# A three-block transformer kernel: norm roots with tokens on partitions, rests one behind, and the sums in front of each norm by two sets of tokens

## The chip, the cores and the metric

The kernel runs on one core of a Trainium2 chip. The metric is the device time of one launch in microseconds (us); lower is better.

## The reference

There are 1024 tokens (`x`, batch 1) and 256 context tokens (`ctx`), with 1024 features each. A first block is followed by an even and an odd layer and a final norm. Cut to what matters here:

```
def rms_norm(x, g):
    return x * rsqrt(mean(x * x, -1) + 1e-6) * g
def modulate(x, cond, g, w, b):        # cond: c for the tokens, c_ctx for the context
    shift, scale, gate = split(silu(cond) @ w + b, 3)
    return rms_norm(x, g) * (1 + scale) + shift, gate

# first block
z = rms_norm(x, g_mix) @ w_in          # four branches are split off it
y_a = chunk_attention(rms_norm(aq), rms_norm(ak), av)           # 4 heads of 64
y_b = indexed_attention(rope(rms_norm(bq)), rope(rms_norm(bk)), bv, iq, rope(rms_norm(ik)), iw)
y_c = rglru(cx, cy)
x = x + (gates * (y_a, y_b, y_c) @ w_branch) @ w_out            # "wo"
gu = rms_norm(x, g_ffn) @ w_ffn_in
x = x + (silu(g) * u) @ w_ffn_out      # 2816 inner features: "fg", "fu", "fo"
# even layer
h, hc = modulate(x, c), modulate(ctx, c_ctx)                    # both give q, k, v and gates
y = (window_attention(8 heads), rms_norm(differential_attention(4 heads)) * 0.2) * silu(g)
x = x + gate * (y @ w_out);  ctx likewise                        # "eo"
# odd layer
h, hc = modulate(x, c), modulate(ctx, c_ctx)
y = (latent_attention(rms_norm(cq), rms_norm(ckv), kr), neighbourhood_attention(8 heads)) * silu(g)
x = x + gate * (y @ w_out)                                       # "oo"
return rms_norm(x, final_g)
```

## The kernel before

**Layout.** Activations lie with features on partitions: `X` is 8 tiles of 128 features by 1024 tokens, plus 256 of context. A projection of one output tile of 128 features takes its tokens in chunks, `CH1` (512, 512) or `CH2` (512, 512, 256), one PSUM bank each. Each product in fp32 is made of three passes (`matmul3`, L2137 to L2139), with the rounded part and the rest of weight and input: 24 matmuls for eight input tiles and 512 tokens. So every input needs its high part (ScalarE) and its rest (VectorE or GpSimd), and every weight tile of 128x1024 too: SP loads it into one of two raw tiles (L2910), ScalarE casts it (L2314), VectorE subtracts (L2481), into one of two slots. `w_get` brings the tile of the next use but one into the slots.

**Order.** `schedule` writes one list of steps in program order; each engine's program walks the whole list and does its part of every step, so an engine is in order throughout, and semaphores tie the engines. Banks 0 to 5 go round in turn (`take`); 6 and 7 are kept for the attentions. In the attentions, a Fill object draws steps of the next head's projections and norms (generators that yield after each piece) between scores and products.

**The norms.** Squares of X are made on ScalarE (L2322) as each output tile of the projection before is added to X (L2678, or L2680 with a gate), and summed over the tiles on VectorE (L2489): `Squares`. When the last tile is there, `norm_split` forms for every chunk a matmul of ones with the sum (L2170, fp32), which puts the mean into all 128 partitions, then a square root on ScalarE (L2325) and a reciprocal on VectorE (L2492), both 128 x 512:

```
p.add("mean", n=n, o=o, ones=ones, x=x, more=list(more), after=list(after), free=bank_free[b])
p.add("root", n=n, rs=rs, ps=ps, after=done, eps=epst[0:rs.shape[0], 0:1] if eps else None)
```

Then come the pieces, eight tiles for each chunk: scale on VectorE (L2501), high part on ScalarE (L2329 to L2335, with the shift where the norm is modulated), rest on VectorE (L2506, L2508) or GpSimd (L2878), by turns. The big norms of this kind are the first one, the feed-forward's (1272), the even layer's (2051) and the odd layer's (3200), all between one block of projections and the next. The context's squares for the even layer are taken behind the feed-forward norm (L2489, 128x256), its pieces with the even layer's norm.

`post` and `post_steps` do the per-head norms of 64 features for queries and keys in the same way (L2170, L2325, L2492, scale L2496), then the rotation (L2179) and the split. `finish_steps` does the norm of a differential head, 128 features by 1280 tokens, three chunks; there the sum has a second term, the squares of the softmax sums, which is added by ten 128x128 matmuls (L2172). The latent attention norms its query and key inputs with `norm_split`. The last norm is done after the last output tile (`final`, L2786 and L2901), with a store for each of 16 pieces.

**Feed-forward.** 22 inner tiles in groups, `FFN_GROUPS = [4, 4, 4, 4, 3, 3]`: for each inner tile the projections `fg` and `fu`, then for the group eight output tiles `fo`, added to X.

**Final projection.** `oo` takes eight input tiles; four of them (`early`) were split before, the other four are split just ahead of it from the last heads' results (`late`), and the projection waits for all.

## Time and profile before

| | |
|---|---|
| median of 3 runs | 4293.37 us (4292.48 to 4294.66) |
| profiled execution | 4297.19 us, span of the trace 4295.4 us |
| granted TensorE clock, mean | 0.923 of full speed |
| busy share | TensorE 83%, weight loads 68%, VectorE 54%, ScalarE 34%, GpSimd 7% |
| matmuls | 18492 |
| VectorE instructions | 3898 |

Times in the rows are microseconds from the span's start. PE is TensorE, PEld its weight load, DVE VectorE, ACT ScalarE, POOL GpSimd; L12 is line 12 of the kernel before; `m` stands for a tile in SBUF and `PS` for one in PSUM. A matmul in fp32 that is not one of `matmul3`'s has two records.

### The profile page before, as it was taken

The page shows a single profiled execution, that of the slowest core. Times are in us where ns is not written, and L with a number is a line of the kernel's source. Part 1 is how long each engine was busy: PE and PEld are TensorE (multiplying, and loading weights), DVE is VectorE, ACT ScalarE, POOL GpSimd, SP SyncE. Part 2 cuts the span into 40 slices and gives each one's busy share as a digit, 9 for nine tenths or more (in the row PEclk, how much of TensorE's full clock was granted, in tenths as well). Part 3 has the DMA queues.
Part 4 walks back from the last instruction along what each step waited for, and adds up shares of the span by engine and source line. Part 5 has one row for each costly group of instructions (what it writes and reads, how often), then busy time and mean ns, then how long its engine had stood idle before and what let it go on. Part 6 is the DMA issues. An engine that isn't in the chain of part 4 may idle for free. (4 is left out here: it accounts for less than half of the span.)

```text
span 4295.4 us, 44938 instructions
## 1 busy us (share of the span) xinstructions
PE 3577.7 (83%) x18492; PEld 2908.7 (68%) x18492; DVE 2309.3 (54%) x3898; ACT 1465.0 (34%) x2564; POOL 296.8 (7%) x379
## 2 busy tenths in 40 slices
PE   3799897786888999999698877877687888868877
PEld 2588775665676888888466665766575777756666
DVE  4899735655733222223565646666544556435654
ACT  3311344443222111112434534444323445324431
POOL 2111110000100000000100000000001000010000
PEclk9899999887998999999799989999798999988998
DMA  2034330001520111111201000000210100100111
GB/s 84 30 108 143 131 133 27 26 20 37 184 88 32 52 49 49 37 45 46 79 27 33 22 31 31 25 26 22 102 69 33 34 29 29 36 23 13 31 64 59
DMA packets 69292, 229.97 MB, mean 54 GB/s; under 512 B 8472, under 2 KB 12568, under 8 KB 69088
## 3 DMA queue, kind: packets, MB, share of 16 engines
q1 hardware_dynamic: 43056, 132.68, 9.3%
q0 software_dynamic: 22576, 81.85, 5.5%
q10 hardware_dynamic: 3456, 12.58, 0.7%
q8 instruction: 145, 2.38, 0.2%
q14 instruction: 59, 0.48, 0.0%
HBM read 180.42 MB, written 36.17 MB: 50 GB/s over the span
## 5 line engine op out<-in xcount | busy, mean ns | idle before, releaser
L2137 PE MATMUL PS<-m,m 128*128 128x512 f32 (+2 forms) x3560 | 1424.5, 401 | 280.4 <-DVE m L2481 55.3
L2138 PE MATMUL PS<-m,m 128*128 128x512 f32 (+2 forms) x3560 | 1379.8, 388 | 0.0
L2139 PE MATMUL PS<-m,m 128*128 128x512 f32 (+2 forms) x3560 | 1379.7, 388 | 0.0
L2137 PEld LDWEIGHTS PS<-m,m 128*128 128x128 f32 (+1 forms) x3560 | 688.6, 194 | 477.1 <-issue 99.9
L2139 PEld LDWEIGHTS PS<-m,m 128*128 128x128 f32 (+1 forms) x3560 | 688.1, 194 | 137.4
L2138 PEld LDWEIGHTS PS<-m,m 128*128 128x128 f32 (+1 forms) x3560 | 690.8, 194 | 120.2 <-issue 3.4
L2481 DVE TENSOR_TENSOR m<-m,m 128x1024 fp32r<-128x1024 f32 (+4 forms) x203 | 207.8, 1024 | 415.0 <-ACT m L2314 414.3
L2766 DVE TENSOR_TENSOR m<-PS,m 128x512 fp32r<-128x512 f32 x352 | 241.1, 689 | 289.3 <-ACT m L2408 288.8
L2408 ACT CAST m<-PS 128x512 fp32r<-128x512 f32 x352 | 205.8, 589 | 512.5 <-PE PS L2236 511.0
L2227 PE MATMUL PS<-m,m 64*128 64x256 f32 (+5 forms) x1968 | 255.6, 371 | 86.2 <-ACT m L2397 57.9
L2227 PEld LDWEIGHTS PS<-m,m 64*128 64x128 f32 (+1 forms) x1968 | 216.8, 200 | 131.1 <-ACT m L2397 73.4
L2314 ACT CAST m<-m 128x1024 fp32r<-128x1024 f32 (+4 forms) x235 | 213.1, 907 | 228.5 <-PE PS L2139 189.0
L2236 PE MATMUL PS<-m,m 128*128 128x128 f32 x1408 | 239.0, 297 | 57.6 <-DVE m L2757 16.0
L2244 PE MATMUL PS<-m,m 128*128 128x256 f32 x704 | 229.2, 345 | 30.7 <-ACT m L2408 15.3
L2236 PEld LDWEIGHTS PS<-m,m 128*128 128x128 f32 x1408 | 180.8, 152 | 103.2 <-DVE m L2766 19.1
L2340 ACT COPY m<-PS 128x512 f32<-128x512 f32 (+1 forms) x158 | 85.5, 543 | 368.8 <-PE PS L2139 368.6
L2397 ACT ACTIVATE m<-PS,m 128x256 f32<-128x256 f32 (+1 forms) x272 | 188.2, 702 | 28.9 <-DVE m L2698 28.9
L2245 PE MATMUL PS<-m,m 128*128 128x256 f32 x704 | 195.4, 297 | 0.0
L2244 PEld LDWEIGHTS PS<-m,m 128*128 128x128 f32 x704 | 145.8, 207 | 43.8 <-ACT m L2408 30.8
L2248 PE MATMUL PS<-m,m 128*128 128x256 f32 x704 | 155.5, 304 | 23.5 <-DVE m L2766 23.1
L2678 DVE TENSOR_TENSOR m<-m,PS 128x512 f32<-128x512 f32 x112 | 76.8, 687 | 180.5 <-PE PS L2139 163.1
L2322 ACT ACTIVATE m<-m 128x512 f32<-128x512 f32 (+1 forms) x133 | 77.5, 594 | 280.1 <-DVE m L2680 169.7
(202 smaller groups left out, 3968.3 us busy)
## 6 DMA issues: line engine op xcount, KB each, us to landing
m<-in_w SPq DMA_DIRECT2D x220, 512.0 KB, 3.3
g_scratch<-m ACTq DMA_DIRECT2D x24, 512.0 KB, 2.6
m<-g_scratch POOLq DMA_DIRECT2D x24, 512.0 KB, 4.7
m<-in_w SPq DMA_DIRECT2D x32, 256.0 KB, 2.6
x_scratch<-m POOLq DMA_DIRECT2D x2, 4096.0 KB, 12.3
m<-m POOLq DMA_DIRECT2D x60, 128.0 KB, 2.7
y_scratch<-m POOLq DMA_DIRECT2D x12, 512.0 KB, 3.0
m<-y_scratch POOLq DMA_DIRECT2D x12, 512.0 KB, 5.4
```

The lines of the kernel that those rows point to most:

```text
L2137: pe.e.engine.matmul(o, L[0], X[0], start=start, stop=False)
L2138: pe.e.engine.matmul(o, L[0], X[1], start=False, stop=False)
L2139: return pe.e.engine.matmul(o, L[1], X[0], start=False, stop=stop)
L2227: m = e.matmul(o, L, X, start=first, stop=last)
L2236: m = e.transpose(PS[:, s["out"] + 128 * i:s["out"] + 128 * i + 128], x, ident)
L2244: e.matmul(O, vh, h, start=g == 0 and i == 0, stop=False)
L2245: e.matmul(O, vl, h, start=False, stop=False)
L2314: e.copy(s["hi"], s["src"]).then_inc(*act.says(S.hi, ("w", s["i"])))
L2397: m = e.activation(d, src if bias is None else d, ACT.Exp, bias=sums[:, 0:1], scale=scale, accum_out=sums[:, 3 + a:4 + a])
L2408: e.copy(s["h"], s["src"]).then_inc(*act.says(S.hi, ("pt", s["u"], s["g"])))
L2481: e.tensor_tensor(s["lo"], s["src"], s["hi"].bitcast(F), ALU.subtract).then_inc(*dve.says(S.lo, ("w", s["i"])))
L2766: e.tensor_tensor(s["l"], s["src"], s["h"].bitcast(F), ALU.subtract).then_inc(*dve.says(S.lo, ("pt", s["u"], s["g"])))
```

## The change

- **Roots with tokens on partitions.** A step "cols" takes 128 tokens of the summed squares as weights and one moving column of constants, so that 128 means land on 128 partitions in one column; root and reciprocal then work on 128 x 4 (or 8, or 10) columns. A step "rows" spreads them again: the column, repeated over 128 columns, is the weight, and the identity moves, which gives a 128x128 block with the roots in every partition. Scale instructions read it from PSUM (banks 6 and 7 for the big norms). All norms are done so, the last and the differential heads' too (there with both terms in the column).
- **Pieces on VectorE and ScalarE.** No rest is left on GpSimd; the shift always goes with the cast; the rest of a piece is issued behind the scale of the next one ("normlo"). The sum of squares is likewise one behind ("sumsq"). The last norm is all on VectorE.
- **Two sets of tokens.** `two_passes` runs the eight output tiles in front of a norm (`wo`, the last `fo` group, `eo`, `oo`) first for tokens 0 to 511 (for `eo` with the context), then again for 512 to 1023, so these weight tiles are loaded and split twice (`weight_order`, 32 more); between the tiles of the second pass the pieces of the first set are issued, two for a tile (three for `eo`). `split_pair` starts the two projections behind the norm on the finished set, issues the second set's columns and pieces at given marks, then finishes both.
- The context's squares and norm for the even layer move between the feed-forward's projections; the groups become [3, 3, 4, 4, 4, 4]; X is loaded in ten parts in place of two (nine in place of eight for `oo`); `oo` takes its early inputs first and waits for each late one alone; the differential heads' fill has one step more.

Cut to its core:

```diff
-FFN_GROUPS = [4, 4, 4, 4, 3, 3]
+FFN_GROUPS = [3, 3, 4, 4, 4, 4]
...
+TWICE = ["wo7", f"fo{len(FFN_GROUPS) - 1}_7", "eo7", "oo7"]
+def weight_order():
+    order = []
+    for tile in weight_tiles():
+        if tile[0][:2] not in ("ea", "oa"):
+            order.append(tile)
+        if tile[0] in TWICE:
+            order += order[-8:]
+    return order
...
-    def linear_steps(name, rhs, chunks, evac, rows=P, banks=None):
-        get, kt, release, split_w = w_get(name)
+    def linear_steps(name, rhs, chunks, evac, rows=P, banks=None, ahead=2, ks=None):
+        get, kt, release, split_w = w_get(name, ahead)
         for n, (t0, tn) in enumerate(chunks):
             b = take(banks)
             o = bank(b)[0:rows, 0:tn]
-            for k in range(kt):
+            for i, k in enumerate(ks or range(kt)):
...
+    def two_passes(jobs, first, then, side, each, **kw):
+        for name, rhs, evac in jobs:
+            linear(name, rhs, first, evac, **kw)
+        for n, (name, rhs, evac) in enumerate(jobs):
+            linear(name, rhs, then, evac, **kw)
+            for _ in range(each if n else 1):
+                next(side, None)
+        finish(side)
...
+    def load_x(X, src, context):
+        t = {(k, 0): move(X[:, k, 0:512], src[k][:, 0:512]) for k in range(8)}
+        c = move(X[:, :, T:TC], ctxT.rearrange("k p t -> p k t")) if context else None
+        e = move(X[:, :, 512:T], src.rearrange("k p t -> p k t")[:, :, 512:T])
+        for k in range(8):
+            t[k, 512], t[k, T] = e, c
+        return t
+    def split_pair(jobs, first, side, marks):
+        done = 0
+        gens = [linear_steps(name, h_rhs, chunks, evac, ahead=2 - n) for n, (name, chunks, evac) in enumerate(jobs)]
+        for n, g in enumerate(gens):
+            for i in range(8 * first[n]):
+                if done == marks[0]:
+                    next(side)
+                if done == marks[1]:
+                    finish(side)
+                done += 1
+                next(g)
+        for n, g in enumerate(gens):
+            for _ in g:
+                pass
+            if n == 0:
+                w_prep(st["use"] + 1)
...
             self.n += 1
-            p.add("square", n=n, x=x, q=self.sq[i][:, 0:tn], r=r, after=list(after) + self.free[i], before=self.t[c])
-            self.t[c] = self.free[i] = [(S.sumsq, n)]
+            p.add("square", n=n, x=x, q=self.sq[i][:, 0:tn], r=None, after=list(after) + self.free[i])
+            self.behind = n, c, i, r, self.sq[i][:, 0:tn]
+        def flush(self):
+            if self.behind:
+                n, c, i, r, q = self.behind
+                self.behind = None
+                p.add("sumsq", n=n, q=q, r=r, before=self.t[c])
+                self.t[c] = self.free[i] = [(S.sumsq, n)]
...
+    def roots(b, tiles, after, width=1, eps=True, at_=None):
+        s = rc_n[0] % 4
+        rc_n[0] += at_ is None
+        d = rc[:, 8 * s:8 * s + width * len(tiles)] if at_ is None else at_[:, 0:width * len(tiles)]
         n = p.id()
-        p.add("mean", n=n, o=o, ones=ones, x=x, more=list(more), after=list(after), free=bank_free[b])
-        return (S.mean, n)
-    def root(rs, ps, b, done, eps=True):
-        n = p.id()
-        p.add("root", n=n, rs=rs, ps=ps, after=done, eps=epst[0:rs.shape[0], 0:1] if eps else None)
+        o = bank(b)[:, 0:width * len(tiles)]
+        p.add("cols", n=n, parts=[(o[:, width * y:width * y + width], terms) for y, terms in enumerate(tiles)],
+              after=list(after), free=bank_free[b])
+        p.add("root", n=n, rs=d, ps=o, eps=epst[:, 0:1] if eps else None, free=rc_free[s] if at_ is None else [])
         bank_free[b] = [(S.root, n)]
-        return (S.recip, n)
-    def norm_split(src, kt, ones, chunks, g, shift, ready, hi, lo, bufs, sums=None):
-        sq, rs, tmp = bufs
+        return n, d, s, width, at_ is None
+    def spread(b, of, y0, tn, m=P):
+        n, d, s, width, shared = of
+        parts = []
+        for y in range(tn // 128):
+            for x in range(width):
+                i, w_ = width * (y0 + y) + x, m // width
+                parts.append((bank(b)[w_ * x:w_ * x + w_, 128 * y:128 * y + 128], d[:, i:i + 1].to_broadcast([P, w_])))
+        x = p.id()
+        p.add("rows", n=x, parts=parts, after=(S.recip, n), free=bank_free[b])
+        if shared:
+            rc_free[s] = [(S.rows, x)]
+        return bank(b)[0:m, 0:tn], (S.rows, x)
...
-        means = []
-        for c, (t0, tn) in enumerate(chunks):
-            b = take()
-            o = bank(b)[:, 0:tn]
-            means.append((b, o, mean(o, ones, rs[c][:, 0:tn], sums.t[c], b)))
-        root_t = [root(rs[c][:, 0:tn], means[c][1], means[c][0], means[c][2]) for c, (t0, tn) in enumerate(chunks)]
-        n, out_events, tmp_free = 0, {}, [[] for _ in tmp]
+        sums.flush()
+        root_of, n = {}, 0
+        chunks = [(c, t0, tn) for c, (t0, tn) in enumerate(chunks) if only is None or c in only]
+        for c, t0, tn in chunks:
+            root_of[c] = roots(take(), by_tiles(rs[c], tn, ones[:, 0:1]), sums.t[c])
+        yield
+        low = []
+        def rest_of():
+            m, key, how = low.pop(0)
+            p.add("normlo", n=m, **how)
+            tmp_free[how["i"]] = out_events[key] = [(S.lo, m)]
+        for c, t0, tn in chunks:
+            b = 6 + norm_n[0] % 2
+            norm_n[0] += 1
+            r, root_t = spread(b, root_of[c], 0, tn)
             for k in range(kt):
                 i = n % len(tmp)
                 sh = shift(k, c) if shift else None
                 m = p.id()
-                p.add("normed", n=m, q=tmp[i][:, 0:tn], x=src(k, t0, tn), g=g(k, c), r=r, sh=sh, how=how, on=on,
-                      hi=hi(k, t0, tn), lo=lo(k, t0, tn), after=[root_t[c]] + tmp_free[i] + ready(k))
-                tmp_free[i] = out_events[k, t0] = [(S.lo if on == "dve" else S.lo_g, m)]
+                q, h = tmp[i][:, 0:tn], hi(k, t0, tn)
+                p.add("normed", n=m, q=q, x=src(k, t0, tn), g=g(k, c), r=r, sh=sh, hi=h,
+                      after=[root_t] + tmp_free[i] + ready(k))
+                low.append((m, (k, t0), {"q": q, "hi": h, "lo": lo(k, t0, tn), "sh": sh, "i": i}))
                 n += 1
-        return out_events
+                if len(low) > 1:
+                    rest_of()
+                if k == kt - 1:
+                    rest_of()
+                yield
+            bank_free[b] = [(S.scale, m)]
...
-                c["m"] = mean(c["o"], cc("o64", c["rows"], c["rows"]), c["x"], [(S.square, n)], c["b"])
+                c["of"] = roots(take(), by_tiles(c["x"], c["tn"], heads(c["rows"])), [(S.square, n)], c["rows"] // 64)
...
-                t = root(c["x"], c["o"], c["b"], c["m"])
+                b = take()
+                r, t = spread(b, c["of"], 0, c["tn"], c["rows"])
                 n = p.id()
-                p.add("scale", n=n, z=c["z"], g=c["gain"][0:c["rows"], :], r=c["x"], after=[t] + c["t"])
-                c["t"] = [(S.scale, n)]
+                p.add("scale", n=n, z=c["z"], g=c["gain"][0:c["rows"], :], r=r, after=[t] + c["t"])
+                bank_free[b] = c["t"] = [(S.scale, n)]
...
+        two_passes([(f"wo{d}", h_rhs, add_to(d, sums)) for d in range(8)], CH1[0:1], CH1[1:2], ffn_norm(0), 2)
...
+                if f0 + f == 0:
+                    split_pair([("fg0", CH1, ev_g), ("fu0", CH1, ev_u)], (1, 1), late_norm(), (3, 7))
+                else:
+                    linear(f"fg{f0 + f}", h_rhs, CH1, ev_g)
+                    linear(f"fu{f0 + f}", h_rhs, CH1, ev_u)
+                if context:
+                    next(context, None)
...
+                two_passes([(f"fo{n}_{d}", u_rhs, add_to(d, sums)) for d in range(8)], CH1[0:1], CH1[1:2],
+                           modulated("ev", bufs, sums, [0]), 2)
...
+        split_pair([("ek", k_first, ek), ("eq0", k_first, eq)], (2, 2), rest, (8, 12))
...
+                of = roots(take(banks), [[(zq[:, 128 * y:128 * y + 128], cc("o128")[:, 0:1]), (ident, squares[h % 2][:, y:y + 1])]
...
+        two_passes([(f"eo{d}", h_rhs, add_gated(d, sums)) for d in range(8)], CH2[0:1] + CH2[2:3], CH2[1:2],
+                   modulated("od", bufs, sums, [0, 2]), 3)
...
+        split_pair([("dq0", CH1, dq), ("dk0", k_first, dk)], (1, 2), rest, (4, 8))
...
+        def final_steps(c):
+            t0, tn = CH1[c]
+            sums.flush()
+            of = roots(take(), by_tiles(rs[c], tn, cc("o1024")[:, 0:1]), sums.t[c])
+            yield
+            r, t = spread(6 + c, of, 0, tn)
             for k in range(8):
+                p.add("final", n=(k, c), x=X[:, k, t0:t0 + tn], r=r, g=vc("fin_g", k), after=t,
                       out=out[k][:, t0:t0 + tn])
+                yield
+        two_passes([(f"oo{d}", y_rhs, add_gated(d, sums)) for d in range(8)], CH1[0:1], CH1[1:2], final_steps(0), 2,
+                   ks=early + [0, 1, 2, 3])
+        finish(final_steps(1))
...
-        elif s.kind == "mean":
+        elif s.kind == "cols":
...
-            m = e.matmul(s["o"], s["ones"], s["x"], start=True, stop=not s["more"])
-            for i, (o, L) in enumerate(s["more"]):
-                m = e.matmul(o, L, ident, start=False, stop=i == len(s["more"]) - 1)
+            for o, terms in s["parts"]:
+                for i, (L, X) in enumerate(terms):
+                    m = e.matmul(o, L, X, start=i == 0, stop=i == len(terms) - 1)
+        elif s.kind == "rows":
+            pe.wait_ge(*s["after"])
+            for ev in s["free"]:
+                pe.wait_ge(*ev)
+            for o, L in s["parts"]:
+                m = e.matmul(o, L, ident, start=True, stop=True)
+            m.then_inc(*pe.says(S.rows, s["n"]))
...
+        elif s.kind == "normlo":
+            dve.wait_ge(S.hi, n)
+            if s["sh"] is None:
+                e.tensor_tensor(s["lo"], s["q"], s["hi"].bitcast(F), ALU.subtract).then_inc(*dve.says(S.lo, n))
+            else:
+                e.scalar_tensor_tensor(out=s["lo"], in0=s["q"], scalar=s["sh"], in1=s["hi"].bitcast(F), op0=ALU.add,
+                                       op1=ALU.subtract).then_inc(*dve.says(S.lo, n))
...
-        elif s.kind == "normed" and s["on"] == "pool":
-            pool.wait_ge(S.hi, n)
-            e.tensor_tensor(s["lo"], s["q"], s["hi"].bitcast(F), ALU.subtract).then_inc(*pool.says(S.lo_g, n))
```

## Rows read from the trace of the kernel before

**Rows 1.** The page, part 1: busy us, share of the span, instructions.

```profile
PE 3577.7 (83%) x18492; PEld 2908.7 (68%) x18492; DVE 2309.3 (54%) x3898; ACT 1465.0 (34%) x2564; POOL 296.8 (7%) x379
```

**Rows 2.** Stretches: length, busy us and records of PE, PEld, DVE, ACT, POOL; clock; DMA, GB/s.

```profile
698.00:1060.00 362.00, 288.12 (x1532) 225.39 (x1531) 221.97 (x460) 170.82 (x316) 19.32 (x50) 0.87 0.06 20
1060.00:1190.00 130.00, 99.71 (x422) 81.65 (x421) 86.01 (x115) 27.82 (x35) 20.02 (x36) 0.87 0.53 189
1190.00:1272.00 82.00, 82.00 (x363) 67.90 (x362) 27.64 (x35) 16.04 (x22) 0.00 (x0) 1.00 0.26 93
1272.00:1322.00 50.00, 25.75 (x54) 13.52 (x53) 32.23 (x34) 18.93 (x31) 12.49 (x10) 0.61 0.00 0
1322.00:2051.00 729.00, 715.14 (x3120) 588.83 (x3119) 214.15 (x285) 129.82 (x193) 0.00 (x0) 0.99 0.15 47
2051.00:2110.00 59.00, 30.50 (x79) 18.94 (x80) 38.86 (x45) 28.05 (x47) 13.97 (x13) 0.65 0.21 80
2520.00:3063.00 543.00, 415.78 (x2496) 345.21 (x2496) 342.09 (x585) 242.89 (x501) 17.07 (x34) 0.92 0.10 31
3200.00:3254.00 54.00, 20.04 (x54) 11.59 (x53) 36.06 (x42) 25.57 (x44) 14.50 (x14) 0.70 0.19 78
```

**Rows 3.** Timeline of VectorE at the end: start, us, instruction, [idle before].

```profile
4263.65 0.75 DVE L2680 SCALAR_TENSOR_TENSOR m<-PS,m,m 128x512 f32<-128x512 f32 x1 [3.30 <-PE PS L2139]
...
4269.09 0.75 DVE L2680 SCALAR_TENSOR_TENSOR m<-PS,m,m 128x512 f32<-128x512 f32 x1 [3.30 <-PE PS L2139]
...
4285.30 6.17 DVE L2786 SCALAR_TENSOR_TENSOR m<-m,m,m 128x512 f32<-128x512 f32 x6
```

**Rows 4.** Timeline of VectorE behind the first block's output projection.

```profile
1275.59 6.56 DVE L2492 RECIPROCAL m<-m 128x512 f32<-128x512 f32 x2 [1.31 <-ACT m L2325]
...
1312.48 0.69 DVE L2506 TENSOR_TENSOR m<-m,m 128x512 fp32r<-128x512 f32 x1 [0.69 <-ACT m L2329]
...
1320.34 1.23 DVE L2481 TENSOR_TENSOR m<-m,m 128x1024 fp32r<-128x1024 f32 x1 [0.51 <-ACT m L2314]
```

**Rows 5.** Groups by form: instruction xcount | busy us, mean ns | idle before.

```profile
L2314 ACT CAST m<-m 128x1024 fp32r<-128x1024 f32 x172 | 179.6, 1045 | 82.3 <-PE PS L2139 43.7 <-DMA m<-in_w 19.7 <-issue 11.6
L2481 DVE TENSOR_TENSOR m<-m,m 128x1024 fp32r<-128x1024 f32 x140 | 171.3, 1224 | 328.9 <-ACT m L2314 328.7
...
L2492 DVE RECIPROCAL m<-m 128x512 f32<-128x512 f32 x38 | 126.6, 3344 | 49.1 <-ACT m L2325 49.0
...
L2759 DVE RECIPROCAL m<-m 128x1 f32<-128x1 f32 x160 | 25.9, 162 | 10.9 <-ACT m L2397 6.8
...
L2680 DVE SCALAR_TENSOR_TENSOR m<-PS,m,m 128x512 f32<-128x512 f32 x32 | 23.9, 751 | 101.8 <-PE PS L2139 75.3 <-DMA m<-in_ctxT 17.7 <-DMA m<-x_scratch 8.8
...
L2492 DVE RECIPROCAL m<-m 128x256 f32<-128x256 f32 x7 | 12.1, 1724 | 0.1
L2496 DVE SCALAR_TENSOR_TENSOR m<-m,m,m 128x512 f32<-128x512 f32 x16 | 12.0, 752 | 0.6
```

**Rows 6.** Timeline of TensorE, narrow matmuls in fp32 at three places.

```profile
522.17 1.84 PE L2206 MATMUL PS<-m,m 128*128 128x2 f32 x16
...
2798.37 1.12 PE L2170 MATMUL PS<-m,m 128*128 128x512 f32 x2 [1.62 <-ACT m L2322]
2799.33 1.05 PE L2172 MATMUL PS<-m,m 128*128 128x128 f32 x8
...
3068.27 1.91 PE L2172 MATMUL PS<-m,m 128*128 128x128 f32 x8
```

**Rows 7.** Timeline of TensorE in the first attention.

```profile
967.99 1.12 PE L2179 MATMUL PS<-m,m 128*128 128x512 f32 x2 [4.09 <-DVE m L2496]
```

**Rows 8.** Timeline of VectorE in the last feed-forward group.

```profile
2041.25 0.55 DVE L2481 TENSOR_TENSOR m<-m,m 128x384 fp32r<-128x384 f32 x1
...
2045.70 0.55 DVE L2481 TENSOR_TENSOR m<-m,m 128x384 fp32r<-128x384 f32 x1
```

**Rows 9.** The page, part 6: count, KB each, median us from issue to landing.

```profile
m<-in_w SPq DMA_DIRECT2D x220, 512.0 KB, 3.3
```

More of the change, by code:

```diff
@@ L857, in w_get @@
         w_load(i + NRAW)
-        w_prep(i + 2)
+        w_prep(i + ahead)
         if i not in parts:
@@ L935, in norm_split, with by_tiles, norm_steps @@
+    def by_tiles(x, tn, X):
+        return [[(x[:, 128 * y:128 * y + 128], X)] for y in range(tn // 128)]
+    norm_n = [0]
+    def norm_split(*args, **kw):
+        out_events = {}
+        for _ in norm_steps(out_events, *args, **kw):
+            pass
+        return out_events
+    def norm_steps(out_events, src, kt, ones, chunks, g, shift, ready, hi, lo, bufs, sums=None, only=None):
+        sq, rs, tmp, tmp_free = bufs
         if sums is None:
@@ L1411, in evac @@
                 x = X[:, d, t0:t0 + tn]
-                p.add("addx", n=n, x=x, o=o, gate=None, after=[done] + t_x)
+                p.add("addx", n=n, x=x, o=o, gate=None, after=[done, t_x[d, t0]])
                 if sums:
```

222 lines of the change are left out of this document (102 added, 120 removed).

## The prediction

> **What bounds the kernel now.** I read the page's first part, then a table of stages, then the timelines of the stages in which TensorE stands still. TensorE is busy for 3577.7 us of 4295.4 [rows 1], so an edit pays only where it closes one of its gaps. The stage table [rows 2] shows where they are. The largest are three boundaries between a block of projections and the next one, at 1272, 2051 and 3200 us: in 50, 59 and 54 us TensorE has 54, 79 and 54 records, of which 48, 72 and 48 are projection work (4, 6 and 6 are the sums' matmuls; the odd ones are neighbours). A projection of 512 tokens by 1024 inputs is 24 matmuls and takes 5.44 us (the distance of two adds that each wait for one, [rows 3]), so the work done in those stretches is 10.9, 13.6 and 10.9 us, and 39, 45 and 43 us are lost. The granted clock there is 0.61 to 0.70, that is, part of the work runs at 1.2 GHz; I put that at 2.6 us for each restart (an estimate: half of 5.3 us in which the restarted projection runs at half pace).
>
> What fills the gaps is VectorE. At 1275.59 two reciprocals of 128x512 take 6.56 us, then come sixteen pieces until 1312.48, then the context's squares, and only at 1320.34 the rest of the next weight, behind which the second projection stands [rows 4]. The reciprocal costs 3344 ns for 512 columns and 1724 for 256, against 0.69 to 0.75 us for every other pass over 512 columns; 47 of them are 145 us of VectorE [rows 5].
>
> **The sums of a norm.** Before, ones(128x128) times the squares gives a full 128x512 sum, rooted (0.69 us) and inverted (3.35). Now four matmuls with one moving column put tokens on partitions, root and reciprocal work on 4 to 10 columns, and four 128x128 matmuls with a constant row spread them. The nearest rows: a pair of records for a matmul with two columns is 2 x 0.115 = 0.23 us (sixteen records in 1.84), a 128x128 matmul in the same number format is 0.26 us at full clock and 0.48 at half [rows 6]. So four columns are 0.9 to 1.0 us, four rows 1.05 to 1.9. Root and reciprocal on a few columns: the reciprocal of one column is 162 ns [rows 5]; I take 0.2 each; bounds 0.15 and 0.7. The chain is thus 2.5 to 3.4 us in place of 2.0 (old matmul, cold) + 0.7 + 3.35, and VectorE gets back 3.2 per chunk.
>
> Where this lies open on the path:
> - Start: two chunks, one behind the other, VectorE setting the pace: 2.2 each, 4. The rests that GpSimd did go to VectorE, which no longer stalls behind it: even.
> - The indexer's key norm: two reciprocals in a row, 5.
> - The first attention's queries and keys (670 to 698): four in a row, 13.4 us (4 x 3.34), and the scores wait for the splits queued behind them. What replaces them ends with the value projection on TensorE (rows 4.3 us longer there): 8.
> - The latent norms (3770 to 3822): five reciprocals (14.8 us), less two spreads at half clock: 10.
> Together 27.
>
> In the attentions twelve chunks are normed between the scores (698 to 1060). VectorE works in order, so each reciprocal holds softmax work: TensorE waited 4.09 us behind the scale that follows one [rows 7], and 2 to 4 behind others. Against it: TensorE now waits itself at the spread until root and reciprocal are through, and does 1.1 us more per chunk. Net 1.7 of 3.35, for twelve 20; bounds 0 and 35. In the differential heads (2520 to 3063) each norm has 8.4 us of reciprocals. Against them stand 20 column matmuls (4.7) and ten rows (2.6) in place of two and a half wide matmuls at 0.96 and ten narrow ones, 5.0 together: 2.3 more, which leaves 6.1. The heads' stream is in places TensorE's own already, so I take a little over half: 3.5 for each of three heads, 3 for the last. Together 34; bounds 5 and 55.
>
> Removed from GpSimd: all rests and the final norm's share; its queue is left with moves. One load of X becomes ten. Nobody waits for them: six banks hold 32 us of projections, and the adds' wait of 17.7 us for the context's load [rows 5] fell between 1190 and 1272, where TensorE was busy for 82 us of 82 [rows 2].
>
> **Two passes at the boundaries.** `two_passes` does all eight output tiles for the first 512 tokens, then all again for the second, with the first half's norm pieces behind the tiles of the second pass. `split_pair` then starts the next two projections on the finished half, while the second half is normed.
> The second half: from the last projection, add 0.75, the sum one behind 0.7, square 0.63, the next weight's two parts in the same queues (1.04 and 1.23, [rows 5]), last sum 0.69: 5 us to the columns, 0.4 to the reciprocal, rows behind the fourth to seventh step, then eight pieces at 1.45 to 1.5 us (scale 0.75, rest 0.7 to 0.75, the cast between them covered because the rest is one behind): done at 21 to 22 us. TensorE has 16.3 us of ready work (19.0 with context) plus 2 of sums, and the last projection can only follow its last piece by 0.7. It loses 6.5, 4 and 4 us.
> The second pass: a tile has one chunk, so 5.44 us of matmuls for a weight of 1.04 + 1.23. VectorE per tile: weight 1.23, add and sum 1.44, two pieces 2.9: 5.6 us, on the edge. Behind a finished tile stand add, sum, pieces, cast, rest until the tile after next may start, 6.6 us: (6.6 + 5.44) / 2 = 6.0 a tile, for four tiles 2.4 us. After the differential layer three pieces go behind a tile: 7.2 a tile, falling to 5.9 with the context's short ones: 6. In the feed-forward's last group (four inputs blocks now, was three) a tile is only 2.72 us and VectorE has 5.1: 9.5 for four tiles, plus 1 of small gaps; before, that group also went at VectorE's pace (4.45 us from one weight rest to the next, [rows 8], against 18 matmuls or 4.08), 3 us.
> Boundaries: 41.6 - 6.5 - 2.4 = 32; 48 + 3 - 4 - 10.5 = 36; 46.3 - 4 - 6 = 36. The columns and rows of the first halves and of the context stand in TensorE's stream, five times 2: -8 (part is hidden where VectorE leads). The context's norm itself moves beside the feed-forward's projections, where VectorE is busy for 214 us of 729 [rows 2]; its two table changes fall on ScalarE's idle time. Without that cover it would be 12.
> 32 more weight tiles on SP's queue: a load lands in 3.3 us [rows 9], and the stage from 1060 moved 189 GB/s [rows 2]; 512 KB in 5.44 us are 96. Nothing, as long as a tile's load, cast and rest stay under 8.6 us (below).
>
> **The last norm.** The final projection starts with the four inputs that are split already and takes the others as they come: 5. After the last add at 4269.09 now follow square, sum, columns, root, rows (4.7 us) and eight scales at 0.7; from the last scale to the end I keep the 3.9 us of before (4291.5 to 4295.4, [rows 3]): the end at 4283.5 for 4295.4, 12.
>
> **Sum.** 27 + 34 + 32 + 36 + 36 - 8 + 5 + 12 = 174 us. The profiled execution took 4297.2 us (1.8 around its span): 4123. The median is 3.8 lower: **4119**.
>
> One price is disputed. The pieces now read the roots from PSUM. The rows with one operand in PSUM and with none are 751 and 752 ns for the same instruction [rows 5], so I charge nothing. The Trainium skill (VectorE: DVE Perf Modes, "The TRN2 errata") gives VectorE 62 cycles more for a PSUM source than for an SBUF one, 65 ns; by an estimate from that page some 130 instructions would lose 8 us, and the time would be 4127 at most. The trace disagrees, and it decides.
>
> **Rivals.**
> A. The attentions keep their waits: TensorE stands at each spread as long as it stood behind the reciprocals. For it: it is in order, and root and reciprocal queue behind exponentials and table loads. Against: 3.35 us of VectorE are gone in any case. 4119 + 34 = 4153. 0.15.
> B. The passes starve. All first-half pieces lie open, because the next weight's rest stands behind them: 24 x 1.45 + 8 x 0.95 = 42 us against the 18 charged: 4143. The stage rows speak for it only in the short last group. 0.10.
> C. More than summed: the attentions give 55, and the restarts at half clock vanish with every short gap: 4090. 0.09.
> D. Slower. Weights come too late for tiles of one chunk. There are 56 such tiles; 174 / 56 = 3.1 us more for each would eat everything, that is 8.6 us per weight, 61 GB/s. The loads' 3.3 us and 189 GB/s speak against. At 10 us a tile the time would be 4370. 0.02.
> E. The halves depend on each other by some wait that I overlooked, so that pieces start after the second pass, and the longer stream of TensorE takes the rest: about 4290. 0.02.
>
> **How the numbers follow.** The forecast has 0.62, its own range 4100 to 4140 (bounds of the attention term and of the pass terms). To leave out no more than 2 in 10 the range takes in most of A, B and C: 4085 to 4162. What this measurement can tell from no change is about 0.2%, 9 us. Faster: forecast, A, B, C, 0.96; same 0.02 (E); slower 0.02 (D).
>
> **What would show it.** No reciprocal over 10 columns under the norms' line; VectorE's busy time down by some 80 us (145 less, rests from GpSimd and weights added); 32 more weight loads of 512 or 256 KB; TensorE's gap at each boundary under 8 us; in the feed-forward's second pass VectorE over 90% for four tiles; after the last projection's end 14 us. Wrong if TensorE waits for a weight's rest in the second passes for more than 20 us in all, or if the spreads in the attentions show waits of 3 us each.

## The result, and the profile after

The changed kernel takes **4178.57 us** (median of 4 runs, 4178.2 to 4181.32) against 4293.48 us; the ratio is 0.9734, 95% interval 0.9717 to 0.9751. That is 115 us less, where 174 were forecast: the right sign, and 4178.6 lies 17 us above the upper end of the range, 4162. The profiled execution has a span of 4176.9 us and took 4178.5.

The page's first part after the change answers to [rows 1]:

```profile
PE 3620.3 (87%) x19222; PEld 2990.5 (72%) x19222; DVE 2210.9 (53%) x3974; ACT 1449.1 (35%) x2556; POOL 242.2 (6%) x344
```

TensorE has 730 records and 42.6 us more than before, and 161 us less of gaps. VectorE fell by 98 us (80 were forecast), in spite of the weights' and pieces' rests it took over.

Stretches after the change (columns as in [rows 2]): the first boundary, the second pass of the last feed-forward group, the second boundary, the differential heads, the final projection's second pass, and the end.

```profile
1248.00:1262.00 14.00, 11.14 (x44) 9.07 (x43) 4.38 (x8) 2.76 (x5) 0.00 (x0) 0.76 0.18 64
1980.00:2012.00 32.00, 24.70 (x107) 18.53 (x108) 23.97 (x37) 14.80 (x23) 0.04 (x1) 0.95 0.22 71
2012.00:2023.00 11.00, 9.41 (x52) 8.10 (x52) 3.01 (x6) 2.21 (x4) 0.84 (x1) 0.84 0.98 357
2443.00:2986.00 543.00, 437.73 (x2601) 370.25 (x2599) 318.47 (x579) 236.20 (x493) 16.98 (x34) 0.88 0.10 31
4104.00:4162.00 58.00, 47.02 (x176) 36.58 (x174) 19.89 (x26) 9.56 (x12) 0.00 (x0) 0.87 0.25 82
4162.00:4177.00 15.00, 3.94 (x16) 3.56 (x16) 7.54 (x12) 0.89 (x2) 0.00 (x0) 0.56 0.37 140
```

The boundaries are closed: 14 and 11 us with 11.1 and 9.4 of TensorE busy, where before 50 and 59 us held 25.8 and 30.5. The end is 15 us. But the last projection's second pass takes 58 us for eight tiles that need 43.5, and the heads' clock is 0.88 where the stage of [rows 2] had 0.92.

To see where the forecast went, one goes through both traces by marks that both have (the last add in front of a norm, the first score of an attention), and takes the lead of the new kernel at each mark.

| up to | before | after | gained in stage | forecast |
|---|---|---|---|---|
| first projection | 65.8 | 55.7 | 10.0 | 4 |
| first top-k step | 171.9 | 160.3 | 1.6 | 5 |
| first attention, first score | 697.6 | 683.5 | 2.5 | 8 |
| its last score | 1042.3 | 1013.5 | 14.7 | 20 |
| last add of `wo` | 1272.2 | 1247.4 | -4.0 | -2.4 |
| last add of the feed-forward | 2053.6 | 2011.0 | 17.8 | 27.6 |
| window attention, first score | 2149.2 | 2068.7 | 37.9 | 44 |
| differential heads, first score | 2515.3 | 2438.8 | -4.0 | 0 |
| their last score | 3049.7 | 2972.8 | 0.4 | 10.5 |
| last add of `eo` | 3199.6 | 3131.0 | -8.3 | -3 |
| neighbourhood attention, first score | 3288.7 | 3179.8 | 40.3 | 42.3 |
| latent attention, first score | 3872.2 | 3753.0 | 10.3 | 10 |
| last add of `oo` | 4269.1 | 4162.0 | -12.1 | 5 |
| end of the span | 4295.4 | 4176.9 | 11.4 | 12 |

(The 8 us for columns and rows stand apart in the forecast.) Three stages make most of the difference: `oo`, 17; the feed-forward with its last group, 10; the heads, 10.

**The final projection.** SP's queue in its second pass, start, us of issue and instruction; and ScalarE's timeline there:

```profile
4113.54 1.00 SPq L3053 DMA_DIRECT2D out<-m  x2
4114.59 0.47 SPq L3046 DMA_DIRECT2D m<-in_w  x1
4122.73 0.99 SPq L3053 DMA_DIRECT2D out<-m  x2
4123.77 0.46 SPq L3046 DMA_DIRECT2D m<-in_w  x1
```

```profile
4118.49 1.04 ACT L2461 CAST m<-m 128x1024 fp32r<-128x1024 f32 x1 [5.20 <-DMA m<-in_w]
...
4127.48 1.04 ACT L2461 CAST m<-m 128x1024 fp32r<-128x1024 f32 x1 [5.36 <-DMA m<-in_w]
```

L3053 are the stores of the last norm's pieces for tokens 0 to 511, L3046 a weight load. Each load is issued only behind two stores, and these wait for scales that come behind the tile's add. The load goes out at 4114.59 and ScalarE waits for it 5.20 us until 4118.49; the tile behind it starts late, and so do its scales and the next load. Four tiles go at 9.0 us.

**The heads.** TensorE's timeline at the column step of the first and of the last head:

```profile
2577.90 6.66 PE L2312 MATMUL PS<-m,m 128*128 128x1 f32 x40 [2.45 <-ACT m L2469]
...
2990.33 8.69 PE L2312 MATMUL PS<-m,m 128*128 128x1 f32 x40 [4.40 <-ACT m L2469]
```

And the granted clock from there on (stretch, length, busy us and records, clock, DMA):

```profile
2578.00:2580.00 2.00, 2.00 (x19) 1.00 0.04 8
2580.00:2582.00 2.00, 2.00 (x12) 0.54 0.00 0
2582.00:2584.00 2.00, 2.00 (x12) 0.50 0.00 0
2600.00:2602.00 2.00, 0.97 (x4) 0.84 0.00 0
2602.00:2604.00 2.00, 2.00 (x11) 1.00 0.00 0
```

20 matmuls with one column (40 records) take 6.66 to 8.69 us, where I had 4.7. At the first head the clock falls to 1.2 GHz at 2580, 2 us into this step, with TensorE busy for 2.00 of 2 us on both sides of the fall (it had waited 2.45 us ahead of the step), and comes back at 2600. At the last head it is at half already ahead of the step (0.52 from 2979 to 2990).

**The last feed-forward group.** VectorE and ScalarE in its first pass:

```profile
1961.90 0.69 DVE L2623 TENSOR_TENSOR m<-m,m 128x512 fp32r<-128x512 f32 x1 [1.27 <-ACT m L2461]
1962.51 0.68 DVE L2820 TENSOR_TENSOR m<-m,PS 128x512 f32<-128x512 f32 x1
1963.11 0.69 DVE L2631 TENSOR_TENSOR m<-m,m 128x512 f32<-128x512 f32 x1
1965.06 0.69 DVE L2623 TENSOR_TENSOR m<-m,m 128x512 fp32r<-128x512 f32 x1 [1.27 <-ACT m L2461]
```

```profile
1963.88 0.63 ACT L2469 ACTIVATE m<-m 128x512 f32<-128x512 f32 x1 [2.02 <-DVE m L2631]
1964.42 0.60 ACT L2461 CAST m<-m 128x512 fp32r<-128x512 f32 x1
```

A tile is 2.72 us of matmuls and goes at 3.16 to 3.22. The square (L2469) waits 2.02 us for the sum of the tile before (L2631), since there is one buffer for squares and the sum now comes one add later; the next weight's cast (L2461) stands behind it, and that weight's rest (L2623) waits 1.27 us for the cast.

### The profile page after: what moved, and what is told of

Read it like the earlier page. It is cut to its first block and busy times, and to the rows that moved or that the text cites. A ratio compares the mean times of both kernels' runs of the same rounds, so it can differ in the third digit from the quotient of the medians.

```text
span 4176.9 us, 46529 instructions
## 1 busy us (share of the span) xinstructions
PE 3620.3 (87%) x19222; PEld 2990.5 (72%) x19222; DVE 2210.9 (53%) x3974; ACT 1449.1 (35%) x2556; POOL 242.2 (6%) x344
## 3 DMA queue, kind: packets, MB, share of 16 engines
q1 hardware_dynamic: 47664, 147.36, 10.8%
## 5 line engine op out<-in xcount | busy, mean ns | idle before, releaser
L2278 PEld LDWEIGHTS PS<-m,m 128*128 128x128 f32 (+1 forms) x3560 | 688.4, 194 | 118.5 <-issue 1.7
L2623 DVE TENSOR_TENSOR m<-m,m 128x1024 fp32r<-128x1024 f32 (+4 forms) x235 | 244.7, 1042 | 474.9 <-ACT m L2461 474.3
L2461 ACT CAST m<-m 128x1024 fp32r<-128x1024 f32 (+3 forms) x267 | 242.5, 908 | 197.8 <-PE PS L2279 132.3
L2391 PE MATMUL PS<-m,m 128*128 128x256 f32 x704 | 223.5, 338 | 34.3 <-ACT m L2553 15.8
L2383 PEld LDWEIGHTS PS<-m,m 128*128 128x128 f32 x1408 | 175.5, 148 | 90.2 <-DVE m L2908 19.3
L2542 ACT ACTIVATE m<-PS,m 128x256 f32<-128x256 f32 (+1 forms) x272 | 188.0, 702 | 19.4 <-DVE m L2840 19.3
L2392 PE MATMUL PS<-m,m 128*128 128x256 f32 x704 | 191.2, 292 | 0.0
L2391 PEld LDWEIGHTS PS<-m,m 128*128 128x128 f32 x704 | 141.8, 201 | 46.6 <-ACT m L2553 34.1
L2469 ACT ACTIVATE m<-m 128x512 f32<-128x512 f32 (+1 forms) x133 | 77.3, 594 | 269.5 <-DVE m L2631 147.6
L2835 DVE TENSOR_REDUCE m<-PS 128x1 f32<-128x1024 f32 x96 | 116.6, 1219 | 101.9 <-PE PS L2374 101.9
L2395 PE MATMUL PS<-m,m 128*128 128x256 f32 x704 | 153.8, 302 | 15.9 <-DVE m L2908 15.8
```

Source lines behind the costliest of these rows:

```text
L2278: pe.e.engine.matmul(o, L[0], X[1], start=False, stop=False)
L2383: m = e.transpose(PS[:, s["out"] + 128 * i:s["out"] + 128 * i + 128], x, ident)
L2391: e.matmul(O, vh, h, start=g == 0 and i == 0, stop=False)
L2392: e.matmul(O, vl, h, start=False, stop=False)
L2461: e.copy(s["hi"], s["src"]).then_inc(*act.says(S.hi, ("w", s["i"])))
L2542: m = e.activation(d, src if bias is None else d, ACT.Exp, bias=sums[:, 0:1], scale=scale, accum_out=sums[:, 3 + a:4 + a])
```

## The experiments

Each starts from the changed kernel (4178.6 us). The runs of one kernel lie 3 to 16 us apart, and stages that an edit doesn't touch differ by 4 to 5 us too (the window attention's took 366 to 371 us in all of them), so I read stages beside medians.

**e1: the stores elsewhere.**

```diff
-        elif s.kind == "final":            # SP
+        elif s.kind == "final" and s["n"][1] == 1:
...
+        elif s.kind == "final" and s["n"][1] == 0:      # GpSimd
+            pool.wait_ge(S.outd, s["n"])
+            e.dma_start(s["out"], s["x"]).then_inc(*pool.says(S.out_g, "stored"))
```

> Edit: the changed kernel, but the last norm's eight stores for tokens 0 to 511 are issued by GpSimd and not by SP. Theory: in the final projection's second pass SP issues each weight load only behind two of these stores (loads at 4114.59, 4123.77, 4132.76 and 4141.79, each 1.05 us behind the first store), so that four tiles take 9.0 us where a tile without stores takes 5.5. Freed of them the four should take 5.5 to 6: 12 to 14 us less, 4165 to 4167 us, and no wait of ScalarE for the weight's load there. Rival: VectorE's and ScalarE's order between scale, add and weight sets the pace, the late load is only where it shows: 4176 to 4180 us.

Measured: 4165.7 us, ratio 0.9702 (0.9688 to 0.9716). From the first to the last add of `oo` it takes 87.6 us for 106.8, 19 less, while the spans of the two profiled executions differ by 16 and the medians by 13. Of the 19, 3 lie in the tile with the columns, ahead of the first of these stores: it takes 8.2 us for 11.3, at a granted clock of 1.00 for 0.70. ScalarE in the same place:

```profile
4113.63 0.63 ACT L2469 ACTIVATE m<-m 128x512 f32<-128x512 f32 x1 [4.99 <-DVE m L2822]
4114.17 1.04 ACT L2461 CAST m<-m 128x1024 fp32r<-128x1024 f32 x1
4120.06 0.63 ACT L2469 ACTIVATE m<-m 128x512 f32<-128x512 f32 x1 [4.85 <-DVE m L2822]
4120.60 1.04 ACT L2461 CAST m<-m 128x1024 fp32r<-128x1024 f32 x1
```

The casts no longer wait. The cause is shown.

**e2: one matmul for the heads' second term.**

```diff
-  of = roots(take(banks), [[(zq[:, 128 * y:128 * y + 128], cc("o128")[:, 0:1]), (ident, squares[h % 2][:, y:y + 1])]
-                           for y in range(10)], [(S.square, n), squares_done[h]], eps=False, at_=inverse)
+  of = roots(take(banks), [[(zq[:, 128 * y:128 * y + 128], cc("o128")[:, 0:1])] for y in range(10)],
+             [(S.square, n), squares_done[h]], eps=False, at_=inverse, wide=(ident, squares[h % 2][:, 0:10]))
...
+  m = e.matmul(*s["wide"], start=True, stop=False)
```

> Edit: the changed kernel, but in the differential heads the second term of the sums (the squares of the softmax sums) is added by one matmul with ten moving columns, and not by ten with one: 11 matmuls in place of 20 in each head's column step. Theory: a column matmul costs 0.33 us here (40 records in 6.66 us), and the granted clock falls to half inside this step (at 2580, TensorE being busy), so each of four heads gives back 3 us and some of the stretch at half clock: 12 to 18 us less, 4161 to 4167 us. Rival: the columns lie beside other waits of the head (the mean of the heads' gaps hides them): 4175 to 4180 us.

Measured: 4163.2 us, 0.9691 (0.9675 to 0.9708), 15 us less. TensorE at the first head's column step:

```profile
2581.98 0.39 PE L2311 MATMUL PS<-m,m 128*128 128x10 f32 x2 [2.45 <-ACT m L2472]
2582.22 2.61 PE L2315 MATMUL PS<-m,m 128*128 128x1 f32 x20
```

The step takes 2.85 us for 6.7 there, and 4.9 in the other heads, where it runs at half clock. From the heads' first score to the last add of `eo` it is 680.2 us for 693.0.

**e3: the heads' norm as before the change.**

```diff
-  r, t = spread(b, of, t0 // 128, tn)
+  p.add("mean", n=m, o=bank(b)[:, 0:tn], ones=cc("o128"), x=r, after=[(S.square, n), squares_done[h]],
+        free=bank_free[b], more=[(bank(b)[:, 128 * y - t0:128 * y - t0 + 128],
+                                  squares[h % 2][:, y:y + 1].to_broadcast([P, P])) for y in tiles])
+  p.add("root", n=m, rs=r, ps=bank(b)[:, 0:tn], eps=None, free=[])
```

> Edit: the changed kernel with the differential heads' norm made as before (a 128x512 mean by a ones matmul and ten narrow ones, root and reciprocal over the full width). Theory: the heads gained nothing by the change (the stage from the first to the last of their scores took 534.4 us before and 534.0 after), so this should be within 4 us of the changed kernel: 4174 to 4183 us. Rival, the predicted price: the columns are worth 13.5 us there, so 4190 to 4194 us.

Measured: 4181.1 us, 0.9737 (0.9723 to 0.9752), the same as the changed kernel; the stage is 691.7 us for 693.0. So at 20 matmuls a head the columns bring nothing, and at 11 (e2) some 12 us (680.2 against 691.7). The mean clock from the heads to `eo` is 0.91 here, 0.86 in the changed kernel and 0.87 in e2, with TensorE busy for 432, 463 and 450 us.

**e4: one pass in front of every norm.**

```diff
-TWICE = ["wo7", f"fo{len(FFN_GROUPS) - 1}_7", "eo7", "oo7"]
+TWICE = []
...
+        if jobs[-1][0] not in TWICE:
+            for name, rhs, evac in jobs:
+                linear(name, rhs, first + then, evac, **kw)
+            finish(side)
+            return
```

> Edit: the changed kernel, but the projections in front of the four norms run in one pass for all tokens, as before; the norm's pieces for the first tokens come behind the last tile, and the pair of projections behind it is still started on them. Theory: the passes cost about what they save. With one pass the boundaries lose 16, 18 and 23 us (6.5 us to the roots, then 16, 16 and 24 pieces at 1.26 to 1.41 us, less the projections they run beside) and the last norm 5, 62 in all; with two passes they lose 12, 20, 15 and 18, 65 in all. So 4165 to 4190 us. Rival, the predicted prices: the passes save what they were charged with, 41 us lost against 62 and more: 4200 us or more.

Measured: 4164.0 us, 0.9698 (0.9683 to 0.9712): **faster than with two passes**, by 15 us, and the intervals don't meet. It is 1 us below the range that I had expected. `split_pair` is still there: the first two projections still start on the first tokens while the others are normed. By stages, in us:

| stage | two passes | one pass | e1 |
|---|---|---|---|
| `wo`, first to last add | 87.9 | 82.3 | 87.9 |
| from there to the first `fo` add | 78.3 | 84.7 | 78.4 |
| `fo`, first to the last group's last add | 685.4 | 670.5 | 688.8 |
| from there to the window attention | 57.0 | 67.9 | 57.1 |
| `eo`, first to last add | 115.0 | 105.6 | 118.5 |
| from there to the neighbourhood attention | 48.0 | 63.7 | 46.4 |
| `oo`, first to last add | 106.8 | 83.8 | 87.6 |
| from there to the end | 14.2 | 19.3 | 13.1 |

The passes save 6.4, 10.9, 15.7 and 5.1 behind the four norms, 38 in all, and cost 5.6, 14.9, 9.4 and 23.0 in front of them, 53. Only `eo` gains, by 6; `wo` is even, the feed-forward's group loses 4, and `oo`, once its stores are out of the way (e1), is 2 us better with two.

**e5: the first attention's norms as before the change.**

```diff
-  r, t = spread(b, c["of"], 0, c["tn"])
+  p.add("mean", n=m, o=o, ones=cc("o64"), x=c["x"], after=[c["sq"]], free=bank_free[b], more=[])
+  p.add("root", n=m, rs=c["x"], ps=o, eps=epst[:, 0:1], free=[])
...
-  p.add("scale", n=n, z=c["z"], g=c["gain"], r=r, after=[t] + c["t"])
+  p.add("scale", n=n, z=c["z"], g=c["gain"], r=c["x"], after=[(S.recip, m)] + c["t"])
```

> Edit: the changed kernel, but the twelve chunks of queries and keys that are normed between the first attention's scores are done as before (full-width mean, root and reciprocal, scale from SBUF). Theory: the columns there are worth what the two traces show between the first and the last of that attention's scores, 14.7 us: 4191 to 4195 us. Rival (TensorE stands at the spreads as long as it stood behind the reciprocals, and the stage gained for other reasons): 4178 to 4183 us.

Measured: 4189.3 us, 0.976 (0.9746 to 0.9775): 11 more, 2 below the range expected. The interval touches that of the changed kernel, so the stage has to decide. From this attention's first score to `wo`'s first add it is 490.6 us for 476.7, 13.9 us, near the 14.7 of the theory; the rest lies in stages that the edit doesn't touch.

**e6: each rest at once.**

```diff
-                if len(low) > 1:
-                    rest_of()
-                if k == kt - 1:
-                    rest_of()
+                rest_of()
```

> Edit: the changed kernel, but the rest of each piece of the big norms is issued right behind its own scale, and not behind the next one's. Theory: VectorE then stands for each cast (0.7 us of wait in each piece, as between the pieces before the change), so the eight open pieces behind each of three boundaries take 2.0 to 2.1 us in place of 1.26 to 1.41, 17 us together, and the second passes, where VectorE is at its edge, lose 5 to 15 more: 4200 to 4212 us. Rival: TensorE has enough ready work to cover it: 4179 to 4188 us.

Measured: 4219.7 us, 0.9828 (0.9813 to 0.9842): 41 more, above my theory's 21 to 33. VectorE behind the first boundary, and the same place in the changed kernel:

```profile
1272.46 0.69 DVE L2645 TENSOR_TENSOR m<-m,m 128x512 fp32r<-128x512 f32 x1 [0.69 <-ACT m L2475]
1273.07 0.74 DVE L2640 SCALAR_TENSOR_TENSOR m<-m,m,PS 128x512 f32<-128x512 f32 x1
1274.50 0.69 DVE L2645 TENSOR_TENSOR m<-m,m 128x512 fp32r<-128x512 f32 x1 [0.69 <-ACT m L2475]
1275.11 0.74 DVE L2640 SCALAR_TENSOR_TENSOR m<-m,m,PS 128x512 f32<-128x512 f32 x1
```

```profile
1251.49 0.68 DVE L2631 TENSOR_TENSOR m<-m,m 128x512 f32<-128x512 f32 x1
1254.31 0.18 DVE L2634 RECIPROCAL m<-m 128x4 f32<-128x4 f32 x1 [2.14 <-ACT m L2474]
1260.25 1.41 DVE L2643 SCALAR_TENSOR_TENSOR m<-m,m,PS 128x512 f32<-128x512 f32 x2 [5.76 <-PE PS L2319]
1261.68 0.69 DVE L2648 TENSOR_TENSOR m<-m,m 128x512 fp32r<-128x512 f32 x1
1262.29 0.74 DVE L2643 SCALAR_TENSOR_TENSOR m<-m,m,PS 128x512 f32<-128x512 f32 x1
1262.95 0.68 DVE L2648 TENSOR_TENSOR m<-m,m 128x512 fp32r<-128x512 f32 x1
```

A piece takes 2.04 us for 1.26. I had left out the start: the first projection begins at 67.4 and not at 55.7, 11.7 us. From the last add of `wo` to the last of the feed-forward it is 14.4 us more, in `eo` 11.8, behind it 7.0.

**e7 and e8: put together.** Both have the edits of e1 and e2. e7 takes the last feed-forward group out of the two passes:

```diff
-TWICE = ["wo7", f"fo{len(FFN_GROUPS) - 1}_7", "eo7", "oo7"]
+TWICE = ["wo7", "eo7", "oo7"]
```

> Edit: the stores on GpSimd, the single matmul for the heads' second term, and the last feed-forward group in one pass. Theory: the first two add up (13 and 15.4 us), and one pass there gives 4 more (14.9 less in the group, 10.9 more behind it, by the trace of the kernel with one pass everywhere): 4143 to 4149 us. Rival: the gains overlap: 4153 us or more.

Measured: **4134.6 us**, 0.9637 (0.9622 to 0.9651), 44 less than the changed kernel, and 8 below the lower end of what I expected. By stages against the changed kernel: the heads with `eo` 13 less, `oo` 19, the feed-forward 16 less and the boundary behind it 10 more. The 6 us that are left are stages that it shares with the others (2 ahead of `wo`, 4 in the window attention).

e8 leaves the two passes there, and gives the squares a second buffer:

```diff
+  bufs = bufs[0], bufs[1], bufs[2][0:3], bufs[3][0:2] + [list(sg_free[0])]
+  sums.sq, sums.free = [bufs[0][0], sg[1]], [sums.free[0], list(sg_free[1])]
```

> Edit: the stores on GpSimd, the single matmul for the heads' second term, and the last feed-forward group in two passes, but with a second buffer for the squares (and three for the pieces in place of four). Theory: with one buffer a square waits for the sum of the one before (2.02 us of wait at each square there), the next weight's cast waits behind it, and the weight's rest behind that, which makes 3.17 us of a tile of 2.72 in the first pass and 5.17 in the second. With two the first pass falls to 2.75 and the second by 0.5 to 1 a tile: 6 to 8 us less than without, 4142 to 4145 us. Rival: another link of the loop holds it, 4148 to 4152 us.

Measured: 4138.1 us, 0.964 (0.9624 to 0.9656), 4 below the range expected, which rested on the same estimate as e7's. VectorE in the group's first pass, for the rows at 1961.90 above:

```profile
1961.41 0.69 DVE L2627 TENSOR_TENSOR m<-m,m 128x512 fp32r<-128x512 f32 x1 [0.61 <-ACT m L2465]
1962.28 0.69 DVE L2824 TENSOR_TENSOR m<-m,PS 128x512 f32<-128x512 f32 x1 [0.18 <-PE PS L2280]
1962.89 0.69 DVE L2635 TENSOR_TENSOR m<-m,m 128x512 f32<-128x512 f32 x1
1964.17 0.69 DVE L2627 TENSOR_TENSOR m<-m,m 128x512 fp32r<-128x512 f32 x1 [0.60 <-ACT m L2465]
```

The tile goes at 2.76 to 2.95, mean 2.86, and the square no longer waits for the sum: that link is shown. The second pass stays at 5.17 with its two pieces, where VectorE has seven instructions and one wait for a cast, so the group gained 2.6 us and not 6 to 8. As a total it can't be told from e7.

**e9: one pass and each rest at once** (the edits of e4 and e6).

> Edit: one pass in front of all four norms, and the rest of each piece right behind its own scale. What of the change is left is the narrow roots, and that VectorE does all rests. Theory: the order of the rests is worth as much with one pass as with two (41 us there): 12 at the start, 0.7 for each of 16, 16 and 24 open pieces, 39, so 4164 + 51 = 4215 us, 4208 to 4222, and again no more than with two passes (4219.7). Rival: slow pieces are where the two passes pay, because more of them lie open in one pass: 4232 us or more.

Measured: 4211.1 us, 0.9801 (0.9787 to 0.9816). So the order of the rests is worth 47 us with one pass and 41 with two, and even with slow pieces the passes don't pay (4211 against 4220). The expectation says that only the narrow roots and the rests on VectorE are left of the change; that is too little. Also left are `split_pair`, the sum of squares one behind, the loads of X in ten parts, the feed-forward's groups and `oo`'s early inputs.

**e10: e7 with `wo` in one pass too.**

```diff
-TWICE = ["wo7", "eo7", "oo7"]
+TWICE = ["eo7", "oo7"]
```

> Edit: as the best so far (stores on GpSimd, single matmul, last feed-forward group in one pass), and the first block's output projection in one pass too. Theory: in the trace with one pass everywhere this projection took 5.6 us less and the stage behind it 6.4 more, so nothing changes: 4132 to 4138 us. Rival: with VectorE freed in front, one pass is better there as well: 4128 us or less.

Measured: 4140.4 us, 0.9634 (0.9618 to 0.965): 2 us above the range, and by its ratio the same as e7. By stages `wo` takes 82.9 us for 87.9 in e7, and from there to the first `fo` add it is 83.7 for 78.2. Even, as e4's stages said.

## Why the prediction was wrong

Taken apart by e9, e4 and the changed kernel, the change is: all that e9 leaves of it (narrow roots, rests on VectorE, `split_pair` and the small parts), 82 us (4293.5 to 4211.1); rests one behind, 47 (to 4164.0); two passes, **minus 15** (to 4178.6). The 82 are not taken apart further: e5 shows 14 of them as narrow roots in the first attention, e3 none in the heads, and no run is without `split_pair`. The forecast of the boundaries themselves came near (37.9 for 44 and 40.3 for 42.3); what stands in front of them was priced far too low, and what closes them was not told apart.

**The step that failed: the price and the worth of the passes.** The sum charged the second passes 2.4, 10.5, 6 and nothing, 19 us. Against one pass they cost 5.6, 14.9, 9.4 and 23.0, 53 us (e4): 34 of the 60 us that the forecast missed. The heads are 10 more. The prediction's own sign came, more than 20 us of TensorE waiting for a weight's rest in the second passes: 1.2, 6.0, 4.6 and 10.9, 22.7 in all. What the passes save, 38, does not pay for it. I had set 39, 45 and 43 us of loss before against what two passes would leave, and never priced the same boundary with one pass and the new pieces. (Of the terms, the third boundary's 46.3 should be 45.7 by the prediction's own numbers; the 36 stands.) I had the numbers: a piece at 1.45 us where before three took 5.8 (one piece in three held by GpSimd's rest). With the 1.26 us measured (e6's rows), sixteen pieces are 20 us, and 11 of these run beside the first two projections, which `split_pair` starts early. Most of what I credited to the passes, the pieces and `split_pair` give without them.

**The final projection, forecast 5, measured -12.** I charged its second pass nothing, neither the 2.4 and 6 us that I charged the others, nor its queue. I counted the loads of a second pass and found them harmless by their rate (96 of 189 GB/s); but the rate was not the limit. SP is in order, the pieces' stores are SP's too, and a load behind a store waits for a scale: 16 us in the tiles behind, 13 in the whole (e1). Rival D had weights that come too late, and had it for all 56 tiles by bandwidth; it happened in four, by order.

**The differential heads, forecast 10.5, measured 0.4.** The reciprocals went, 8.4 us a head. The term that was mis-sized is the columns: 0.23 us each from a row at full clock [rows 6], 0.33 measured and up to 0.43, because the clock is at half for 4.4 of the 6.66 us at the first head, and for all of the 8.69 at the last. I had looked at both clocks for the rows and at one for the columns. With nine matmuls fewer (e2) the stage takes 525.7 us, 9.1 less than before, near the forecast.

The columns are not needed to bring the clock down. At the first head of e2 it falls 2 us behind the start of the step, as in the changed kernel, but at the third it falls inside the wait, which ends at 2864.48 with the step's first matmul. TensorE in e2 there, and in e3, where the same norm has waits of 1.63, 1.21 and 0.99 us between wide matmuls until 2591:

```profile
2862.00:2864.00 2.00, 0.03 (x2) 1.00 0.00 0
2864.00:2864.40 0.40, 0.00 (x0) 0.61 0.00 0
```

```profile
2583.00:2592.00 9.00, 5.56 (x30) 1.00 0.01 2
```

So a wait of 2.45 us was enough without a column, and with the shorter waits the clock stayed up through the sums. Whether the columns add to it is open.

**The last feed-forward group, forecast -7.5, measured -13.9.** It takes 60.4 us (1950.6 to 2011.0) for 43.5 of matmuls, 16.9 lost for 3 before. The second pass came as said, at VectorE's pace: 5.17 us a tile for 5.1. The first pass I had at TensorE's pace; one buffer for the squares made it 3.2 for 2.72, 3.1 us over eight tiles, of which a second buffer gives back 2.0 (e8). The trace before could not show this link: there a square waited for its add only (1.4 us, L2678), and the sum stood right behind it. The one buffer began to hold when the change put the sum one behind.

**The start, forecast 4, measured 10.** I had called the rests even; one behind, they give 11.7 us (e6), as much as the whole gain there.

**The small norms.** Head norms of 64 features need two row matmuls for 128 tokens: in front of the first attention 64 records, 3.71 us, ahead of the last value projection, where the prediction had 4.3. The reciprocals' 13.4 us are gone, and the scores start only 2.5 us earlier in the stage, for 8; what took the other 5.5 no run shows. In the attention itself 14.7 for 20, within its bounds, and shown (e5).

**What was right.** The boundaries' own gaps: at the second, 57.7 us from the last add to the first score hold 40.8 of projections and 10.8 that both kernels have (a copy's wait, transposes), so 6 are lost, where I had 4 and the columns. Before it was 95.6 us, 44 lost and not 48. The latent norms, 10 for 10; the odd layer's boundary, 40 for 42; the end, 11.4 for 12; no price for reading the roots in PSUM, by the rows below. Rival A did not come: at all spreads together TensorE is idle for 12 us (8.8 and 2.9, below). Rival B came half: the passes in front of the first three norms cost 30 us, where the forecast had 18 and the rival 42.

Groups by form after the change: instruction, count, busy us, mean ns, idle before.

```profile
L2643 DVE SCALAR_TENSOR_TENSOR m<-m,m,PS 128x512 f32<-128x512 f32 x70 | 51.3, 744 | 23.2 <-PE PS L2319 23.0
L2312 PE MATMUL PS<-m,m 128*128 128x1 f32 x284 | 50.6, 308 | 64.8 <-DVE m L2631 49.3 <-ACT m L2469 15.5
...
L2319 PE MATMUL PS<-m,m 128*128 128x128 f32 x204 | 43.6, 385 | 8.8 <-DVE m L2922 5.0 <-DVE m L2634 3.8
...
L2319 PE MATMUL PS<-m,m 128*64 128x128 f32 x272 | 24.4, 327 | 2.9 <-DVE m L2908 2.6 <-DVE m L2634 0.3
...
L2312 PE MATMUL PS<-m,m 128*128 128x2 f32 x128 | 19.2, 272 | 8.5 <-ACT m L2469 6.1 <-DVE m L2908 2.3
```

The scale with one operand in PSUM takes 744 ns, for 752 with none [rows 5]. So the table of the Trainium skill (VectorE: DVE Perf Modes, "The TRN2 errata") that gives VectorE 120 cycles of fixed cost from PSUM and 58 from SBUF, 62 more, is not borne out here. The 8 us that I had estimated from it were not seen in these instructions.

## What to carry to other kernels

When a change closes a gap in two ways at once, price the gap with each alone: here the cheap half (a better order of VectorE's pieces, and projections started on half of the tokens) had already closed most of it, and the dear half (each weight twice) cost more than it still found. Work that is moved beside other work moves its DMA issues too: in an in-order queue a store that waits for a result holds every load behind it, whatever the bandwidth. And for many tiny matmuls behind a wait count both clocks.

## What the runs showed of the hardware

- The clock fell from 2.4 to 1.2 GHz while TensorE was busy, 2 us into a run of one-column matmuls behind a wait of 2.45 us, and 20 us at half clock followed. In e2 it fell inside such a wait of 2.45 us (granted 1.00 until 2864.0, 0.61 from there to 2864.4), before any column; in e3, with waits of 1.63, 1.21 and 0.99 us, it stayed at 1.00.
- A one-column matmul with 128x128 weights in fp32 takes 0.26 us at full clock (1.05 us for four) and 0.43 at half (8.69 for twenty). A 128x128 one takes 0.26 at full clock too (1.05 for four), so between 1 and 128 columns their number made no difference there.
- A reciprocal of four columns takes 0.18 us, for 3.34 with 512.
- VectorE's instructions that wait for nobody start 0.60 to 0.66 us apart where each is 0.69 to 0.75 long, so a chain of them is some 12% shorter than the sum of their durations; a piece took 1.26 us where the sum is 1.43.
